# FFN down projection of nine passes as seven block products instead of eight

## What is computed

```python
D_MODEL, FFN_DIM = 1024, 2816
def swiglu_half(x, pre, post, w_gate, w_up, w_down):
    h = rmsnorm(x, pre)
    y = (jax.nn.silu(h @ w_gate) * (h @ w_up)) @ w_down
    return x + 0.5 * rmsnorm(y, post)
```

## Time and profile before

| what | value |
|---|---|
| median of 3 runs | 3251.58 us |
| profiled execution, its own time | 3251.07 us |
| its span, first to last instruction | 3249.4 us |
| PE busy, PEld busy | 96%, 90% of the span |
| DVE, ACT, POOL busy | 51%, 29%, 9% |
| matmuls of line 1557 (gate-up and down of both FFNs) | 9504 of 25814 |
| DMA, mean | 67 GB/s |

### The profile page before, as it was taken

One profiled execution on the slowest core, in us unless ns is written; L12 is line 12 of the kernel. 1 busy time (PEld: TensorE's weight loads), 2 busy tenths in 40 slices (PEclk: granted clock), 3 DMA queues, 4 the chain that ended last, 5 costly groups with the idle time before them and its releaser, 6 DMA issues. The chain is left out here.

```text
span 3249.4 us, 61897 instructions
## 1 busy us (share of the span) xinstructions
PE 3103.7 (96%) x25814; PEld 2936.3 (90%) x25814; DVE 1655.5 (51%) x2929; ACT 939.9 (29%) x1754; POOL 299.8 (9%) x338
## 2 busy tenths in 40 slices
PE   7999999999999989988899989999999999999998
PEld 7999999998899988847777569999998999999998
DVE  4454444546544746666554453344435554455545
...
DMA packets 257467, 218.58 MB, mean 67 GB/s; under 512 B 41688, under 2 KB 235009, under 8 KB 256634
## 3 DMA queue, kind: packets, MB, share of 16 engines
...
q10 hardware_dynamic: 1040, 0.00, 0.0%
...
## 5 line engine op out<-in xcount | busy, mean ns | idle before, releaser
L1557 PE MATMUL banks<-XR,wR 128*128 128x344 f32 x6336 | 1006.1, 320 | 6.1 <-DVE rs L1671 4.1
L1557 PEld LDWEIGHTS banks<-XR,wR 128*128 128x128 f32 x6336 | 1000.2, 189 | 6.7 <-issue 3.3
L1557 PE MATMUL banks<-hidR,wR 128*128 128x344 f32 x3168 | 510.9, 321 | 2.9 <-DVE tiles L1791 2.9
L1557 PEld LDWEIGHTS banks<-hidR,wR 128*128 128x128 f32 x3168 | 500.5, 188 | 9.2 <-DVE tiles L1791 4.6
L1640 ACT ACTIVATE sq<-sq 128x344 f32<-128x344 f32 x120 | 59.2, 493 | 926.9 <-DVE sq L1669 926.9
L1691 DVE TENSOR_TENSOR tiles<-tiles,banks 128x344 f32<-128x344 f32 x480 | 240.8, 512 | 165.6 <-PE banks L1557 164.8
L1167 PE MATMUL banks<-XR,pR 128*128 128x344 f32 (+1 forms) x1944 | 318.2, 325 | 3.6 <-DVE pR L2281 2.9
L1167 PEld LDWEIGHTS banks<-XR,pR 128*128 128x128 f32 (+1 forms) x1944 | 311.5, 190 | 10.2 <-issue 6.1
L1167 PE MATMUL banks<-XR,mg_gate 128*128 128x344 f32 x1728 | 283.3, 319 | 1.3 <-PEq L53 1.3
L1167 PEld LDWEIGHTS banks<-XR,mg_gate 128*128 128x128 f32 x1728 | 273.9, 188 | 1.6 <-issue 1.6
L1669 DVE TENSOR_TENSOR sq<-banks,shared 128x344 f32<-128x344 f32 x120 | 62.0, 516 | 365.6 <-PE banks L1557 365.5
...
## 6 DMA issues: line engine op xcount, KB each, us to landing
wraw<-in_ffn_down SPq DMA_DIRECT2D x22, 1024.0 KB, 4.9
wraw<-in_ffn_gate SPq DMA_DIRECT2D x43, 512.0 KB, 3.7
wraw<-in_ffn_up SPq DMA_DIRECT2D x43, 512.0 KB, 4.7
praw<-in_w_in SPq DMA_DIRECT2D x26, 512.0 KB, 4.2
...
sq<-in_w_in SPq DMA_DIRECT2D x24, 512.0 KB, 4.0
...
```

The lines of the kernel that those rows point to most:

```text
L1557: ins = self.k.nc.tensor.matmul(out, wgt[:, a, cols], x(b)[:, grp(g)], start=first and n == 0, stop=last and n == 2)
```

## The change

Passes 2 to 10 of each FFN (nine turns of a loop, `SevenProducts`) do the down projection in another way. For two hidden tiles and the tokens in two halves of 516, it is a product of 2 x 2 blocks (output tiles j and j + 4 by hidden tile; hidden tile by token half), and Winograd's form of Strassen's scheme gives it in seven block products instead of eight, with sums taken of the blocks beforehand and of the products afterwards. Block names: A11, A21, A12, A22 of the weights with the sums S1 to S4; B11, B21, B22 of the hidden values with the mixes T1 to T4. A job (c, j) is one quarter j of the output tiles and one of two pieces c of 258 tokens of each half: seven products of three matmuls of 258 tokens each. There are eight jobs a pass.

- Gate-up groups are of 258 tokens, (t, q) with q = 0 to 3: eight groups of 48 matmuls instead of six.
- PE's order in a turn is: group (0,0), pair 0, group (0,1), pair 1, group (0,2), pair 2, groups (0,3), (1,0), (1,1), (1,2), (1,3), pair 3. A pair is two jobs. Pair 3 belongs to the turn's own hidden values, pairs 0 to 2 to those of the turn before; behind the last turn stand pairs 0 to 2 alone.
- Per job, ACT copies products 1, 2 and 4 out of PSUM (c1, t2, t4), DVE does six additions (c2, p5a, p5b, c3, p3, s12) and later a seventh (s22), and POOL four (a1, a2, a4, a3). POOL also makes the mixes T1 to T4 and the weight sums S1 to S4. High and low parts are made of the mixes and the weight sums too (`high`, `low`, `weights_high`, `weights_low`).
- Weights land in the low half of their place in `wR` (`wlow`), after the last matmul that used it, and ACT and DVE split them there.

The core of the diff:

```diff
+    ORDER = (1, 2, 6, 5, 4, 7, 3)
+    JOBS = ((0, 2), (0, 3), (1, 0), (1, 1), (1, 2), (1, 3), (0, 0), (0, 1))
+    READER = {1: "c1", 2: "t2", 6: "c2", 5: "p5b", 4: "t4", 7: "c3", 3: "p3"}
+    BY_ACT, BY_DVE, BY_POOL = ("c1", "t2", "t4"), ("c2", "p5a", "p5b", "c3", "p3", "s12"), ("a1", "a2", "a4", "a3")
+    WEIGHT = {1: 0, 2: 2, 4: 3, 7: 1, 5: 4, 6: 5, 3: 6}
+    HIDDEN = {1: "B11", 2: "B21", 3: "B22", 4: "T4", 5: "T1", 6: "T2", 7: "T3"}
...
+    def down(self, pe, pair, turn):
+        if pair == 3:
+            self.dve_s.wait(pe, ("w", "sums"), turn)
+            self.dve_s.wait(pe, ("low", "D", 0), turn)
+        if pair == 1:
+            self.dve_s.wait(pe, ("low", "D", 1), turn)
+        for c, j in self.jobs(pair):
+            for i in self.ORDER:
+                at = self.place((c, j), i) - 4
+                user = (self.READER[self.ORDER[at % 7]],) + self.JOBS[at // 7]
+                (self.act_s if user[0] in self.BY_ACT else self.dve_s).wait(pe, user, turn, int(at < 0))
+                for x, (a, b) in enumerate(((0, 0), (0, 1), (1, 0))):
+                    ins = self.k.nc.tensor.matmul(self.bank((c, j), i), self.weight(i, a, j), self.part[b][self.HIDDEN[i]][c],
+                                                  start=(x == 0), stop=(x == 2))
+                self.pe_s.done(ins, (i, c, j))
...
+    def evict(self, act, pair, turn, hidden=True, products=True):
+        out_of = {"c1": (1, self.c1), "t2": (2, [self.t2] * 2), "t4": (4, [self.t4] * 2)}
+        for step in self.evicted[pair]:
+            x, c, j = step
+            if x == "sig" and hidden:
+                self.sigmoid(act, c, j, turn)
+            elif x == "sig" or not products:
+                self.act_s.skip(act, [step], turn)
+            else:
+                last, before_last = self.earlier((c, j), 1), self.earlier((c, j), 2)
+                if x == "c1":
+                    self.dve_s.wait(act, ("c2",) + before_last[0], turn, before_last[1])
+                    self.pool_s.wait(act, ("a1",) + before_last[0], turn, before_last[1])
+                else:
+                    self.pool_s.wait(act, ("a2" if x == "t2" else "a4",) + last[0], turn, last[1])
+                i, out = out_of[x]
+                self.pe_s.wait(act, (i, c, j), turn)
+                self.act_s.done(self.k.nc.scalar.activation(out[j % 2], self.bank((c, j), i), ACT.Copy), step)
+    def high(self, act, x, c, turn):
+        if x == "A":
+            self.pool_s.wait(act, ("T1", c), turn)
+        elif x == "B":
+            self.dve_s.wait(act, ("h", 1, 2 * c + 1), turn)
+        else:
+            self.pool_s.wait(act, ("T3", c), turn)
+        self.act_s.done(self.k.nc.scalar.activation(self.wide[0][x][c], self.wide_raw[x][c], ACT.Copy), ("hi", x, c))
...
+    def once_on_act(self, act, turn):
+        first = isinstance(turn, int)
+        for q in range(3):
+            self.evict(act, q, turn, products=not first)
+            if q == 1:
+                self.high(act, "A", 0, turn)
+                self.weights_high(act, "gu1", turn)
+        self.sigmoid(act, 0, 3, turn)
+        self.high(act, "A", 1, turn)
+        self.sigmoid(act, 1, 0, turn)
+        self.weights_high(act, "gu0", turn)
+        self.weights_high(act, "down", turn)
+        self.sigmoid(act, 1, 1, turn)
+        self.weights_high(act, "sums", turn)
+        for x in "BCD":
+            self.high(act, x, 0, turn)
+        self.sigmoid(act, 1, 2, turn)
+        self.evict(act, 3, turn)
+        for x in "BCD":
+            self.high(act, x, 1, turn)
...
+    def low(self, dve, c, turn):
+        for x in "ABCD":
+            self.act_s.wait(dve, ("hi", x, c), turn, c)
+            if x == "A":
+                self.pool_s.wait(dve, ("T2", c), turn, c)
+            if x == "B":
+                self.pool_s.wait(dve, ("T3", c), turn, c)
+            self.dve_s.done(self.k.nc.vector.tensor_tensor(self.wide[1][x][c], self.wide_raw[x][c],
+                                                           self.wide[0][x][c].bitcast(F32), ALU.subtract), ("low", x, c))
...
+    def add_up(self, dve, pair, turn):
+        k, add = self.k, self.k.nc.vector.tensor_tensor
+        for c, j in self.jobs(pair):
+            job = (c, j)
+            at = slice(HALF + c * PIECE, HALF + (c + 1) * PIECE)
+            top, low, c3 = k.A[:, j, at], k.A[:, 4 + j, at], self.c3[j % 2]
+            last = self.earlier(job, 1)
+            self.dve_s.wait(dve, ("s12",) + last[0], turn, last[1])
+            self.act_s.wait(dve, ("c1", c, j), turn)
+            self.pe_s.wait(dve, (6, c, j), turn)
+            self.dve_s.done(add(self.c2, self.c1[j % 2], self.bank(job, 6), ALU.add), ("c2", c, j))
+            self.pe_s.wait(dve, (5, c, j), turn)
+            self.dve_s.done(add(low, low, self.bank(job, 5), ALU.add), ("p5a", c, j))
+            self.dve_s.done(add(top, top, self.bank(job, 5), ALU.add), ("p5b", c, j))
+            self.pe_s.wait(dve, (7, c, j), turn)
+            before_last = self.earlier(job, 2)
+            self.pool_s.wait(dve, ("a3",) + before_last[0], turn, before_last[1])
+            self.dve_s.wait(dve, ("c2", c, j), turn)
+            self.dve_s.done(add(c3, self.c2, self.bank(job, 7), ALU.add), ("c3", c, j))
+            self.pe_s.wait(dve, (3, c, j), turn)
+            self.dve_s.wait(dve, ("p5b", c, j), turn)
+            self.dve_s.done(add(top, top, self.bank(job, 3), ALU.add), ("p3", c, j))
+            self.dve_s.wait(dve, ("p3", c, j), turn)
+            self.dve_s.done(add(top, top, self.c2, ALU.add), ("s12", c, j))
...
+    def once_on_dve(self, dve, turn):
+        first = isinstance(turn, int)
+        for q in range(3):
+            self.gated(dve, 0, q, turn)
+            if first:
+                self.skip(dve, self.dve_s, self.BY_DVE, q, turn)
+            else:
+                self.add_up(dve, q, turn)
+            self.hidden(dve, 0, q, turn)
+            if first:
+                if q == 0:
+                    self.dve_s.skip(dve, [("low", x, 1) for x in "ABCD"], turn)
+                self.skip(dve, self.dve_s, ("s22",), q, turn)
+            else:
+                if q == 0:
+                    self.low(dve, 1, turn)
+                self.add_rest(dve, q, turn)
+            if q == 1:
+                self.weights_low(dve, "gu1", turn)
+        for t, q in ((0, 3), (1, 0)):
+            self.gated(dve, t, q, turn)
+            self.hidden(dve, t, q, turn)
+        self.weights_low(dve, "gu0", turn)
+        self.gated(dve, 1, 1, turn)
+        self.hidden(dve, 1, 1, turn)
+        self.weights_low(dve, "down", turn)
+        self.weights_low(dve, "sums", turn)
+        self.gated(dve, 1, 2, turn)
+        self.hidden(dve, 1, 2, turn)
+        self.low(dve, 0, turn)
+        self.gated(dve, 1, 3, turn)
+        self.add_up(dve, 3, turn)
+        self.hidden(dve, 1, 3, turn)
+        self.add_rest(dve, 3, turn)
...
+    def carry_over(self, pool, pair, turn):
+        k, add = self.k, self.k.nc.gpsimd.tensor_tensor
+        for c, j in self.jobs(pair):
+            at = slice(c * PIECE, (c + 1) * PIECE)
+            top, low = k.A[:, j, at], k.A[:, 4 + j, at]
+            self.act_s.wait(pool, ("c1", c, j), turn)
+            self.pool_s.done(add(top, top, self.c1[j % 2], ALU.add), ("a1", c, j))
+            self.act_s.wait(pool, ("t2", c, j), turn)
+            self.pool_s.wait(pool, ("a1", c, j), turn)
+            self.pool_s.done(add(top, top, self.t2, ALU.add), ("a2", c, j))
+            self.act_s.wait(pool, ("t4", c, j), turn)
+            self.pool_s.done(add(low, low, self.t4, ALU.add), ("a4", c, j))
+            self.dve_s.wait(pool, ("c3", c, j), turn)
+            self.pool_s.wait(pool, ("a4", c, j), turn)
+            self.pool_s.done(add(low, low, self.c3[j % 2], ALU.add), ("a3", c, j))
+    def mix(self, pool, c, turn):
+        raw, sub = self.raw, self.k.nc.gpsimd.tensor_tensor
+        self.dve_s.wait(pool, ("h", 1, 2 * c + 1), turn)
+        self.pool_s.wait(pool, ("T1", c), turn)
+        self.pool_s.done(sub(raw["T2"][c], raw["B22"][c], raw["T1"][c], ALU.subtract), ("T2", c))
+        self.pool_s.wait(pool, ("T2", c), turn)
+        self.pool_s.done(sub(raw["T4"][c], raw["B21"][c], raw["T2"][c], ALU.subtract), ("T4", c))
+        self.pool_s.done(sub(raw["T3"][c], raw["B22"][c], raw["T3"][c], ALU.subtract), ("T3", c))
+    def weight_sums(self, pool, turn):
+        sub = self.k.nc.gpsimd.tensor_tensor
+        pool.wait_ge(self.ffn.landed["down"].sem, (turn + 2) * 16)
+        self.pool_s.done(sub(self.S1, self.A21, self.A22, ALU.add), ("S", 1))
+        self.pool_s.wait(pool, ("S", 1), turn)
+        self.pool_s.done(sub(self.S2, self.S1, self.A11, ALU.subtract), ("S", 2))
+        self.pool_s.wait(pool, ("S", 2), turn)
+        self.pool_s.done(sub(self.S4, self.A12, self.S2, ALU.subtract), ("S", 4))
+        self.pool_s.done(sub(self.A21, self.A11, self.A21, ALU.subtract), ("S", 3))
...
+    def once_on_pool(self, pool, turn):
```

(29 more changed lines are left out.)

317 lines of the change are left out of this document (269 added, 48 removed).

## The result

The changed kernel takes 3294.67 us (median of 4 runs, 3290.28 to 3297.39), the kernel before 3253.71 on the same chip (4 runs, 3251.31 to 3259.21): ratio 1.0128, 95% interval 1.0114 to 1.0141. It is slower by 41 us. The profiled execution of the change, the slowest of its four, took 3297.39 us, 46.3 more than that of before.

What follows compares the result with a forecast made beforehand. PE bounds the passes: number of matmuls times their pace. Fewer columns save 2.7 us a pass, but waits make a turn 69.5 against 68.2; with lone pairs and clock +42 on 3251.07: 3293 us, 8 in 10 from 3236 to 3345.

Steps and rivals of the forecast that it cites:

- Pace: PE's matmuls of 258 tokens take 118.7 ns, from a line through two sizes; a pass takes 65.5 us without waits.
- Pair 2: In each turn PE's seventh product waits for c2, behind gu1's low part on DVE; 2.4 us with 0.2 at the second job.
- Ahead of pair 3: Low parts of down and sums alternate with T2, T4, T3, ending at 23.65 against 22.8 due: 1.1 us a turn.
- Pair 1 and pair 0: Pair 1's low parts come just in time, 0; pair 0's fifth product gets its bank late, 0.3 us a turn.
- PE's 0.2 per job and the free bank absorb: Argument against every s12 costing PE time: slack inside a pair absorbs the first s12 blocked by a POOL addition.
- The port: DVE operations with both operands in SBUF and POOL's work alternate, one at a time: 62.6 us of it in 65.5.
- first rival: DVE and POOL hinder each other little; pair 2 still waits 1.6, pair 3 nothing; turn 67.4, 3254 us; chance 0.18.
- The lone pairs: Behind the last turn, without a group to hide beside: 6.0 idle in pair 0, pair 2 ends at 29.9 us per FFN.
- The clock: Idle in the lone pairs may drop it to its lower level, 1.2 GHz: 2 us per FFN (0 to 5).
- The sum: Per FFN 632.6 us against 613.8, twice 37.6 more; with the lower clock together +42, giving 3293 us.
- pair 2 not held: Rival: DVE is through with gu1 by 12.2, so c2 of pair 2 isn't late: 3219 us; chance 0.13.
- Heavier: Rival: every s12 loses a full POOL addition, a pair costs about 1 us, a turn 73.5: 3373 us; chance 0.13.

Runs made afterwards that it cites:

- waits product by product: Changed kernel, with products of pairs 3 and 1 waiting for low parts A, B, C, D one by one instead of for D ahead of the first: 3277.79 us.
- narrow additions: Changed kernel, with POOL's a1 to a4 on 4 columns in place of 258, the rest left out of the result: 3279.86 us.
- a3 behind s12: a3 waits for s12 of its job instead of c3, against a kernel with four edits and the last gu1 split first (3245.75): 3237.53 us.
- gu1 moved: Changed kernel, with DVE making gu1's low part behind pair 2 instead of between pairs 1 and 2: 3269.98 us.

## Why the prediction was right, and where its steps were off

The forecast was 3293 us, slower, by waits of PE in pair 2, ahead of pair 3 and in the lone pairs. All three are there, in other sizes: 25 us in pair 2 (16 turns), 14 ahead of pair 3 (18 turns) and 30 in the lone stretches with their clock (35.85 + 34.5 against 20.2 each without waits), where the forecast had 38, 20 and 24. The profile says 46.3 us more where the sum said 42. Its terms, point by point:

**Pace.** 118.7 ns from the line through 256 and 344 columns. Measured 119.8 (240 matmuls from 333.50 to 362.25 in the run with waits product by product). With the products' starts 0.35 to 0.37 apart the turn without waits is 66.2, not 65.5: 6 us in eight turns of an FFN, the largest miss on the slow side. The columns gave 1.9 us a pass (613.35 / 9 is 68.15), not 2.7.

**Pair 2.** 2.4 forecast, 1.58 measured. The chain is the one that was walked, member by member: h ends 8.00 us behind pair 1's start (walked 8.15), T1 8.94 (9.05), A 9.6 (9.8), gu1 11.4 and 13.7 (11.7, 14.0), c2 starts at 13.99 (14.4). It ran 0.4 early in the end, 0.1 of it where ACT's second step began ahead of the first one's end (330.04 against 330.14). And pair 2 started at 11.12, not 10.7, for the slower pace and pair 1's 0.3. Both shorten the wait: 0.8 a turn, as much on the fast side as the pace on the slow one.

**Ahead of pair 3.** 1.1 forecast, 0.77 measured. DVE's and POOL's rows of the changed kernel:

```profile
357.51 2.28 DVE L2165 TENSOR_TENSOR wR<-wlow,wR 128x2048 fp32r<-128x2048 f32 x1
357.67 2.72 POOL L2272 TENSOR_TENSOR mixed_raw<-hid_raw 128x258 f32<-128x258 f32 x1 [5.55 <-DVE hid_raw L2147]
...
359.71 2.30 DVE L2165 TENSOR_TENSOR down_sums<-down_sums_raw,down_sums 128x1536 fp32r<-128x1536 f32 x1
360.47 2.14 POOL L2274 TENSOR_TENSOR rs<-hid_raw,mixed_raw 128x258 f32<-128x258 f32 x1
...
367.25 0.42 DVE L2156 TENSOR_TENSOR mixed_last<-rs,mixed_last 128x258 fp32r<-128x258 f32 x1
```

T2 ends 0.60 behind DVE's low part (360.39, 359.79), and DVE's next, 1.76 by the line, ends 1.62 behind T2: they take turns, as walked. The last low part ends 23.6 us behind group (0,3), where 23.65 was walked; the group before pair 3 ended 0.2 to 0.3 later than thought, for the slower pace, and that is the difference. No run took POOL's mixes out of this stretch: that the port has a share in this wait is read from the rows and not tested.

**Pair 1 and pair 0.** That "PE's 0.2 per job and the free bank absorb" a blocked s12 was wrong for pair 1: s12 loses to a3, c2 of the second job follows it, and PE waits 0.33; the narrow additions and a3 behind s12 both show it. The 0.3 in pair 0 is 0.03, and a lead of 0.01 us of s12 over a3 keeps it so.

**The port.** What it does to a blocked instruction was right, how many are blocked and its weight in the sum too high. Of the means that were to be well above their price, s12 (620 ns), silu (630), s22 (558) and POOL's a1 (873 against 760) are; h (428), a3 (797), a2 and a4 (688, 696) are not. Without the additions the turn falls by 0.61; the forecast stood 2.1 above its first rival. The stalls of a turn, 2.8, lie between the forecast's 4.0 and that rival's 1.9, nearer to the rival's: with the measured pace the forecast's turn would have been 70.2 and the rival's 68.1, and 69.05 is halfway. That the time fell beside the forecast and not between the two is luck, in that the pace missed the other way. The same holds for the Trainium skill, "SBUF — State Buffer", section "Who interferes with whom": its rule fits s12's 620 against 428 ns here, but what decided was the order of instructions in DVE's own queue, which the rule says nothing of.

**The lone pairs.** 29.9 + 2 forecast, 35.85 and 34.5 measured. The waits are 4.8 in pair 0 and 3.7 ahead of pair 1 (starts against due times) for 6.0 and 3.4, and 1.5 in pair 2 for 0.4. The clock is the step that was sized too small. PE's timeline in FFN 1:

```profile
724.86 1.01 PE L2021 MATMUL banks<-mixed_last,wR 128*128 128x258 f32 x3 [4.63 <-ACT sq L2080]
725.67 0.85 PE L2021 MATMUL banks<-mixed,wR 128*128 128x258 f32 x3
...
734.16 1.66 PE L2021 MATMUL banks<-hidR,wR 128*128 128x258 f32 x6 [3.58 <-DVE mixed_last L2156]
735.62 0.85 PE L2021 MATMUL banks<-mixed,down_sums 128*128 128x258 f32 x3
```

After each of the two waits the products are 0.65 apart instead of 0.355. Seven from 724.86 to 729.36 and nine from 734.16 to 739.80 took 10.1 us for 5.7: 4.4 us, not 2, though inside the range of 0 to 5 that the text gave it.

**The sum.** Turns 7 us less than forecast in both FFNs (552.7 for 556.0), first turns 2.6 more, lone pairs 6.5 more, 1 from the passes of before being 613.3 and not 613.8, 1.2 outside the passes: 42 becomes 46. The size is right partly because misses of opposite sign cancel, and that is luck; the mechanism of pair 2 and of the wait ahead of pair 3 is shown by the runs that undo it. The rivals: "pair 2 not held" (3219) needed DVE free of gu1 by 12.2; it was through at 13.7, and with gu1 moved the wait went, as this rival has it. "Heavier" (3373) has its place right, s12 behind a POOL addition, but at 0.33 us once a turn instead of 1 us a pair.
